# First feed-forward blocks and retention's gated values: transposes moved from TensorE to VectorE blocks and a DRAM trip issued by ScalarE

## What is computed

```python
# first block, each layer: feed-forward with squared relu, D_FF = 4096
m = jnp.square(jax.nn.relu(jnp.einsum('bsd,df->bsf', m, w_up[i])))
m = jnp.einsum('bsf,fd->bsd', m, w_down[i])
# second block, each layer: a gated feed-forward before and after the mixer, D_FF_2 = 2816
gate, up = jnp.split(u @ w_in, 2, axis=-1)
return (jax.nn.silu(gate) * up) @ w_out
# retention in the mixer: 4 heads with values of width 512
out = out * lax.rsqrt(jnp.mean(out * out, axis=-1, keepdims=True) + EPS)
ob = (jax.nn.silu(g) * ret.reshape(Bsz, S, RET_V).astype(u.dtype)) @ w_ret_out
```

## Time and profile before

| | |
|---|---|
| median of 3 runs | 2319.97 us (2319.95 to 2320.0) |
| span of the profiled execution | 2318.0 us; the page gives no time of its own for that execution, and the median lies 1.97 us above the span |
| TensorE busy | 2296.8 us, 99% of the span |
| VectorE busy | 1540.9 us, 66% |
| ScalarE busy | 1221.5 us, 53% |
| DMA | 188 GB/s in the mean, 434.91 MB |
| granted TensorE clock | 0.999 in the mean |

### The profile page before, as it was taken

How to read it: one execution, slowest core, us unless ns; L and a number is a source line. 1 busy time by engine, 2 the same in 40 slices (tenths; PEclk the granted TensorE clock), 3 DMA queues, 4 the chain that set the end, 5 groups by cost and what they waited for, 6 DMA issues and landing times.

```text
span 2318.0 us, 30390 instructions
## 1 busy us (share of the span) xinstructions
PE 2296.8 (99%) x12124; PEld 1959.9 (85%) x12124; DVE 1540.9 (66%) x2019; ACT 1221.5 (53%) x1788; POOL 79.1 (3%) x134
## 2 busy tenths in 40 slices
PE   8999999999999999999999999999999999999998
PEld 6888888888888888988888888888889888888887
DVE  6867657776566667876575665665678765756664
ACT  6645446464455556755444554554567553445553
POOL 0110000100000000000000000000000000000000
PEclk9999999999999999999999999999999999999999
DMA  8437655456656555645665465565556456554652
GB/s 334 146 119 238 198 171 209 146 170 203 211 163 217 189 172 163 206 162 183 218 199 191 157 217 192 179 221 190 173 164 214 153 183 221 195 193 164 199 193 89
DMA packets 119805, 434.91 MB, mean 188 GB/s; under 512 B 13553, under 2 KB 13809, under 8 KB 119665
## 3 DMA queue, kind: packets, MB, share of 16 engines
q1 hardware_dynamic: 119664, 432.96, 56.4%
HBM read 431.86 MB, written 1.05 MB: 187 GB/s over the span
## 4 chain that ended last, share of the span: by engine, by line
PE 95%; DVE 4%; ACT 1%; issue 0%; POOL 0%; DMA 0%; DVEq 0%; POOLq 0%; ACTq 0%
PE ub L1716 21%; PE ub L1713 11%; PE ub L1684 9%; PE ub L1686 9%; PE ub L1685 9%; PE acc L1684 8%; PE acc L1685 8%; PE acc L1686 8%; PE ub L1691 1%; PE ub L1692 1%; PE ub L1693 1%; PE acc L1747 1%; DVE wlo L1020 1%; DVE work L1208 1%; PE acc L2162 0%; DVE best L1205 0%
## 5 line engine op out<-in xcount | busy, mean ns | idle before, releaser
L1020 DVE TENSOR_TENSOR wlo<-raw,whi 128x1024 fp32r<-128x1024 f32 x776 | 913.1, 1220 | 215.2 <-ACT whi L534 213.4
L534 ACT ACTIVATE whi<-raw 128x1024 fp32r<-128x1024 f32 x776 | 777.3, 1052 | 200.9 <-PE ub L1686 140.5
L1716 PE MATMUL ub<-xhl,whi 128*128 128x512 f32 x2176 | 514.6, 390 | 0.0
L1716 PEld LDWEIGHTS ub<-xhl,whi 128*128 128x128 f32 x2176 | 404.2, 188 | 82.7 <-issue 1.3
L1684 PE MATMUL acc<-whi,bhl 128*128 128x512 f32 x736 | 288.2, 392 | 0.0
L1685 PE MATMUL acc<-wlo,bhl 128*128 128x512 f32 x736 | 286.6, 389 | 0.0
L1686 PE MATMUL acc<-whi,bhl 128*128 128x512 f32 x736 | 286.5, 389 | 0.0
L1684 PE MATMUL ub<-whi,xhl 128*128 128x512 f32 (+1 forms) x704 | 275.3, 391 | 3.0 <-DVE wlo L1020 1.5
L1713 PEld LDWEIGHTS ub<-xhl,wlo 128*128 128x128 f32 x2176 | 272.0, 191 | 6.2
L1713 PE MATMUL ub<-xhl,wlo 128*128 128x256 f32 x2176 | 275.4, 283 | 0.0
L1686 PE MATMUL ub<-whi,xhl 128*128 128x512 f32 (+1 forms) x704 | 272.5, 387 | 0.0
(11 more groups left out here) (305 smaller groups left out, 2471.7 us busy)
## 6 DMA issues: line engine op xcount, KB each, us to landing
raw<-in_w SPq DMA_DIRECT2D x776, 512.0 KB, 5.0
gain<-in_gains SPq DMA_DIRECT2D x20, 512.0 KB, 7.8
tapw<-in_taps SPq DMA_DIRECT2D x16, 512.0 KB, 4.3
DEC<-in_decay SPq DMA_DIRECT2D x2, 768.0 KB, 8.1
par<-in_par SPq DMA_DIRECT2D x2, 647.0 KB, 9.4
par<-in_par SPq DMA_DIRECT2D x2, 556.0 KB, 7.2
H<-in_x SPq DMA_DIRECT2D x2, 512.0 KB, 4.5
out_h<-H SPq DMA_DIRECT2D x4, 256.0 KB, 2.6
```

The source lines that it names most:

```text
L534: do(act.activation(whi[:, s % RING, c], raw[:, slot, c], ACT.Copy), counts["w_hi"])
L1020: do(dve.tensor_tensor(wlo[:, s % RING, c], raw[:, PLACES[s][0], c], whi[:, s % RING, c].bitcast(f32), ALU.subtract), counts["w_lo"])
L1716: last = pe.matmul(bank, whi[:, s % RING, n:n + P], xhl[:, kt, :, :].rearrange("p a n -> p (a n)"), start=first, stop=stop, skip_group_che ...
```

## The change

The turns by TensorE go away. In their place:

1. VectorE turns each 128 x 512 tile in SBUF as 4 x 16 blocks of 32 x 32 (`to_blocks`, one STREAM_TRANSPOSE), from `FH` into the new `FB`, or from `tX` into `PB[:, hd]`, which lies over the values `Vhi` of that head (so `Vhi` and `Vlo` are now laid out by heads). It sets `blocked` or `pb`.
2. ScalarE waits for that, and issues on its own queue one DMA of the whole buffer to a DRAM tensor (`put`): 1 MB in the first feed-forward, 512 KB in a gated one and for each head.
3. ScalarE waits for the end of that DMA (`put`) and issues four DMAs back (`get`), of which each gathers 32 partitions from 4 places of 2 KB or 1 KB a row. They bring the blocks to the partitions where they belong.
4. ScalarE waits for these (`moved0` or `moved1`), and rounds from SBUF into `bhi` (`first_hi`, `turned_p`); VectorE writes the rest into `blo` (`rest_of`).

In the feed-forwards put stands at the end of up 4, get at the end of up 5, and `first_hi` with `first_lo` at the end of up 6. `hid_of` asks for 7 and 5. In the first one two more ups now stand ahead of down 0, so that it follows up 8 and not up 6. In retention of head hd: put at the next g, get one g later, `turned_p` one head later. Counted over the program, 128 transposes of TensorE go, 32 of VectorE come, and 14 turns come with 5 DMAs each, 70 in all.

```diff
 def ffn1_order():
-    seq = [("first", j) for j in range(4)] + [("up", 4), ("up", 5), ("up", 6)]
-    for j in range(9):
-        seq += [("down", j), ("up", j + 7)]
-    return seq + [("down", j) for j in range(9, 16)]
+    seq = [("first", j) for j in range(4)] + [("up", j) for j in range(4, 9)]
+    for j in range(7):
+        seq += [("down", j), ("up", j + 9)]
+    return seq + [("down", j) for j in range(7, 16)]
...
+                def put(event, src):
+                    issued[event] += 1
+                    act.wait_ge(sem[event], issued[event])
+                    g = issued["put"]
+                    issued["put"] += 1
+                    act.dma_start(turned_rows[g * P:(g + 1) * P, 0:src.shape[1]], src).then_inc(sem["put"], 16)
+
+                def get(dst):
+                    g = issued["get"]
+                    issued["get"] += 1
+                    act.wait_ge(sem["put"], 16 * (g + 1))
+                    n = dst.shape[1] // 4
+                    for c in range(4):
+                        act.dma_start(dst[32 * c:32 * c + 32, :].rearrange("j (a x) -> j a x", a=4),
+                                     turned_rows[g * P:(g + 1) * P, c * n:(c + 1) * n].rearrange("(a j) x -> j a x", a=4)
+                                     ).then_inc(sem[f"moved{g % 2}"], 16)
...
                         elif kind == "g":
                             hd = j // 2
-                            if j % 2 == 0:
-                                if hd:
-                                    turned_p(hd - 1)
-                            else:
+                            if j % 2 == 0 and hd:
+                                put("pb", PB[:, hd - 1, :])
+                            if j % 2:
                                 used(s)
+                                act.wait_ge(sem["pb"], RET_HEADS * L + hd)
...
                                 squares_o(hd)
+                                if hd:
+                                    get(PB[:, hd - 1, :])
+                                if hd >= 2:
+                                    turned_p(hd - 2)
                         elif kind == "ya":
                             if j == 0:
-                                turned_p(RET_HEADS - 1)
+                                put("pb", PB[:, RET_HEADS - 1, :])
...
+                            if j == 0:
+                                get(PB[:, RET_HEADS - 1, :])
+                            if j in (0, 2):
+                                turned_p(2 + j // 2)
...
+                def to_blocks(dst, k, n, source, count=None):
+                    return do(dve.transpose(in_blocks(dst, k, n), source.rearrange("p (q c i) -> p q c i", c=4, i=32)), count)
...
+                        if (kind, j) in (("g", 6), ("ya", 0), ("ya", 1), ("ya", 3)):
+                            turned_p(dict(g=0, ya=1)[kind] + (j + 1) // 2 * (kind == "ya"))
...
                     if event == "pd":
-                        return max(j + 1, 5)
-                    return max(2 * j, 3)
+                        return max(j + 1, 7)
+                    return max(2 * j, 5)
```

More of the change, by code:

```diff
@@ L270, in build @@
         rb = acc[:, 3, S:S + PAIRS]
+        turned_rows = nc.dram_tensor("turns", (16 * P, 2048), f32, kind="Internal").ap()
         names = ("x_in0 x_in1 cst_in cst2_in pos_in posi_in par_in p_in decay_in g_in0 g_in1 w_in0 w_in1 w_in2 w_in3 w_in4 w_in5 w_in6 w_in7 out_done w_hi w_lo split_free "
@@ L776, in _ @@
                                 positive(1, 1)
-                                first_hi(((0, 0), (1, 0)))
                         elif kind == "up":
@@ L785, in _ @@
                             if j == 4:
-                                first_hi(((0, 1), (1, 1)))
+                                put("blocked", FB[:, :])
+                            elif j == 5:
+                                get(FB[:, :])
+                            elif j == 6:
+                                first_hi(2)
                         else:
@@ L846, in ffn @@
                                 if j == 4:
-                                    first_hi(((0, 1),))
+                                    put("blocked", FB[:, 0:1024])
+                                elif j == 5:
+                                    get(FB[:, 0:1024])
+                                elif j == 6:
+                                    first_hi(1)
                             else:
@@ L1494, in gated_values @@
                                                         ALU.mult, ALU.mult), counts["rp"])
+                        settle()
+                        for t in range(2):
+                            to_blocks(PB[:, hd, :], t, 2, tX[:, t, :], counts["pb"] if t else None)
                     def turned_p(hd):
@@ L1586, in _ @@
                                 decayed(0)
-                            elif j % 2 == 0:
-                                turned_p(hd - 1)
-                            elif hd + 1 < RET_HEADS:
+                            elif j % 2 and hd + 1 < RET_HEADS:
                                 decayed(hd + 1)
@@ L1797, in take @@
                             fill(U_[2 * b + t], "fp")
-                    def turn_first(b, t):
-                        pe.wait_ge(sem["fp"], fp0 + (t if gated else 2 * t + b) + 1)
-                        A_[2 * b + t].take(pe, sem["hid"], hid0 + (2 * t + 1 if gated else 3 * t + b + 1))
-                        for q in range(4):
-                            last = pe.transpose(acc[:, 2 * b + t, q * P:(q + 1) * P],
-                                                FH[:, 2 * b + t, q * P:(q + 1) * P], ident)
-                        give(last, "tr_done")
                     halves(s0, lambda b, t: ub[:, 2 * b + t, :], take, turned0, "fa")
@@ L1810, in ffn @@
                         s = s0 + n
-                        if kind == "first":
-                            if j == 3:
-                                for b in range(1 if gated else 2):
-                                    turn_first(b, 0)
-                        elif kind == "up":
+                        if kind == "up":
                             pair(s, j % 2, event)
-                            if j == 4:
-                                for b in range(1 if gated else 2):
-                                    turn_first(b, 1)
-                        else:
+                        elif kind == "down":
                             pe.wait_ge(sem["hid"], hid0 + hid_of(j, event))
```

112 lines of the change are left out of this document (60 added, 52 removed).

## The result

The changed kernel takes **2339.39 us** (median of 4 executions, 2337.05 to 2341.15) against 2319.97 us: a ratio of 1.0083, 95% interval 1.0070 to 1.0097, so it is slower by 19.4 us. The forecast was 2317.0 us with a range to 2331 us. The profiled execution took 2339.55 us, its span is 2337.7 us, 19.7 us longer than before.

The account below looks back on a forecast made before the run. TensorE, busy in 99% of the span, was taken as the bound. Terms -14.2 + 8.2 + 2.6 + 0.4 = -3.0 us gave 2317.0 us on the median, with a range of 2306 to 2331 us.

Parts of the forecast that it names:

- What is taken from TensorE: All mixers and feed-forwards: removing TensorE's batches of transposes saves 14.2 us in all.
- Block transpose 0.69 us: VectorE's new block transpose, priced like an addition of 512 columns, between bounds of 0.42 and 1.2 us.
- retention up to ya0 at nothing: Mixers, from g7 back to g1: the new work fits beside TensorE's 14.3 us a head and costs nothing.
- order at nothing: First feed-forward: ups and downs moved past each other, same number and kind, cost nothing.
- A DMA issue, 0.47 us of ScalarE: Each put or gather issue takes 0.47 us of ScalarE, as on SyncE; ends 0.1 and 0.9 us.
- ya0 to gb0, +8.2 us: Both mixers: TensorE waits 3.6 us before ya3 and 0.4 us more before gb0, 4.0 to 4.1 us twice.
- First feed-forward, +2.6 us: Two first feed-forwards: put and gathers share engines with SyncE's loads, so down 0 waits 1.3 us, twice.
- Gated, +0.4 us: Four gated feed-forwards: get hardly waits for put, margin 0.5 us before up 9, counted 0.1 us each.
- Rival (c), the clock: TensorE's clock falls in the forecast's stalls, losing 1.5 us after each of two: +3 us, 2320.0 us; chance 0.06.
- Rival (b): Slower: issues take longer on ScalarE than SyncE, before ya1's and up 6's copies; at 0.9 us 2332.5 us; chance 0.22.
- Rival (d): The way back is slow for its strides; gathers landing 5 us later give +26 us, 2343 us; chance 0.03.

Follow-up runs that it names:

- c3_later3: Changed kernel with earlier put and get in feed-forwards, mixers' rounding and rest one block earlier, head 3's get behind ya3's rounding: 2307.22 us.
- a4_no_trip: Changed kernel without put and get, so blocks are never exchanged and the output differs: 2307.13 us.
- c2_order: Kernel before the change with only the new order of the first feed-forward's ups and downs: 2319.89 us.
- d1_put_early: Changed kernel with put alone moved ahead of up 4's copy in all feed-forwards, get left in place: 2331.16 us.
- b1_early: Changed kernel with the feed-forwards' put ahead of up 4's copy and get earlier too, rounding left in place: 2313.62 us.
- b4_double: Changed kernel with each of get's four gathers split into two of half the rows, eight issues for the same bytes: 2367.41 us.
- a1_ret: Kernel before the change with only retention's gated values turned the new way: 2320.20 us.
- a3_gated: Kernel before the change with only the four gated feed-forwards turned the new way: 2330.26 us.

## Why the prediction was wrong

- **What is taken from TensorE**: right; -14.2 against 14.0 us of busy time (c3_later3) and 13.2 us (a4_no_trip).
- **Block transpose 0.69 us, retention up to ya0 at nothing, order at nothing**: right (0.67 to 0.71 us; no wait in g1 to g7; c2_order within the interval).
- **A DMA issue, 0.47 us of ScalarE**: the size was right (0.31 to 0.71 us, 0.45 in the median; eight in 3.87 us). Where ScalarE has slack the issues cost nothing, as in the first feed-forward, where put even went out ahead of a chunk and a rounding written before it.
- **ya0 to gb0, +8.2 us**: the right place and too large: 2.04 + 0.39 and 1.71 + 0.38 = 4.5 us. The gathers of head 2 were issued beside g7's squares (from 1057.98 both) and those of head 3 beside ya0's rounding (1069.29 both), where I had counted one after the other.
- **First feed-forward, +2.6 us: the step that failed most.** I let put share the engines and land at 182.3, and the gathers land by 190.0 "by the same rate". Put landed 4.3 us after its issue, by 176; the gathers were issued at 178.1 to 179.9 and the last landed at 192.9. So put's leg was 6.3 us shorter than priced, and the gathers' leg 14.8 us instead of 7.7. The waits were 4.34 and 5.26 us in place of 1.3. I had priced the gathers by bytes at half of 361 GB/s, as if their turn came at once. They got no packet for 3 us and then 99 GB/s (0.99 MB in 10 us); d1_put_early and b1_early show that what counts is whether they are issued ahead of or behind SyncE's burst. By the Trainium skill, page "DMA: Bandwidth & Descriptors", section "Rules for kernel authors", a DMA is to be issued early and its semaphore waited on late; by that rule put and get belonged earlier, with the rounding where it was, and b1_early agrees (25.8 us less). The page's rule on the 16 shared engines, which the prediction weighed (Trainium skill, the same page, section "Issuing engines are not separate DMA queues"), held as well: a queue of ScalarE's own gave its gathers no room beside SyncE's loads, they shared the engines (33.6% and 70.4%).
- **Gated, +0.4 us: failed as badly.** The term rested on "get stands at 726.1 and need hardly wait". Put's price, 4 to 5 us, was taken from a load in the stream; it took 7.8 us in the first gated one, 2.7 us past the point where ScalarE needed it. I had written that beyond the margin of 0.5 us all comes through, four times, and that is what came: 1.39, 1.89, 2.34 and 2.74 us.
- **Rival (c), the clock** had 0.06. It was 8.1 us behind four waits. It followed from the waits: behind waits of the length that came it belonged into the sum, not beside it as a rival. 1.5 us each was near for two of them (1.6 and 1.4) and too little for two (2.7 and 2.4). Its 3 us at the lower level stood on no row; at down 0 the matmuls started 0.43 us apart for 5.3 us.
- **Rival (b)**, the only one with a slower result and weight, had the wrong mechanism (the issue's price), and its 2332.5 us fell short too. **Rival (d)** named late gathers, at 0.03, put down to their strides; they were late, but not for that in the main (b1_early).

Sum by measured terms: transposes -14.2, mixers +4.5, first feed-forwards +9.6, gated +8.4, clock +8.1: +16.4 us of the profile's 19.7. The split rests on one profiled execution of each kernel. The remaining 3.3 us stay open; part may be what each of ten waits costs beyond the row's figure, since a matmul's row lasts 0.39 us and the next would start after 0.23.

## What to carry to other kernels

A transfer that shares the DMA engines with a stream of loads is to be priced by what the other queue has in flight when it is issued and by the share that its own packets get beside it, not by its bytes alone: look where the other queue bursts, and issue before that. A trip through DRAM is cheap when put follows its data at once, get stands where the issuing engine has slack, and the use is several blocks later; no issue may stand ahead of a sum that the bounding engine waits for. And a forecast stall of TensorE of about 2 us may carry a second term, for the clock; here each one of 2.3 us and more did.

## What the runs showed of the hardware

- Rows of one engine's DMA issues can stand ahead of compute instructions written before them (put at 171.65, the chunk ahead of it in the code at 171.95), and delay the ones after them only when the stream is behind (b4_double, 3.29 us idle at 1086.23). That each engine's stream is strictly in order, as the text ahead of the prediction has it, is true of the compute rows shown and not of these issues.
- Behind SyncE's burst the first packet of four gathers ran over 3 us after their first issue (none from 178 to 181 us). Then the two queues ran almost one packet for one (547 and 590 from 182 to 192 us), so the queue with packets of half the size moved half the bytes (0.99 and 2.15 MB).
- After its rise at the start, the granted clock fell to 0.50 behind every wait of TensorE of 2.3 us and more in the profiled kernels. Behind waits of 1.8 to 2.2 us it fell in some (2.01 and 1.81 us before ya3 in b1_early) and not in others (2.04 us at the same place in the changed kernel, 2.17 and 1.99 us in a1_ret). Sixteen matmuls whose result is dropped kept it at 1.00.
- Executions of one kernel can differ by 9.5 us: a3_gated took 2323.79 to 2333.31 us at mean clocks of 0.999 to 0.997, where before spread by 2.4 us. Executions at the same 0.999 differed by 5.7 us, so the clock is not the whole reason; what else differed was not profiled.
